# Hybrid decoder layer with expert retrieval, one core: the four-tap convolutions of blocks 1 and 2 move from VectorE to GpSimd

## What is computed

```python
def _causal_dwconv(x, buf, w):                 # width 4 for lru_x
    full = jnp.concatenate([buf.astype(x.dtype), x], axis=1)
    y = full[:, 0:s] * w[0]
    for k in range(1, width):
        y = y + full[:, k:k + s] * w[k]
    return y, full[:, full.shape[1] - (width - 1):]
...
    xc, new_lru_buf = _causal_dwconv(xl, lru_buf, lp['lru_conv_w'])
    xc = xc + lp['lru_conv_b']
    r = jax.nn.sigmoid(... w_rg_a ...); i = jax.nn.sigmoid(... w_rg_x ...)
    h = _linear_scan(a, bt, h0)                # bt uses i * xc
...
        act = jax.nn.gelu(jnp.einsum('td,thkd->thk', xb, u_tab[e]))
        return jnp.einsum('thk,thkd->td', g * act, v_tab[e])
```

## Time and profile before

| | us |
|---|---|
| three runs of the kernel | 3116.53, 3113.41, 3114.4 |
| their median | 3114.4 |
| the profiled execution, its time | 3113.92 |
| its span, first to last instruction | 3112.1 |

### The profile page before, as it was taken

How to read it: one execution, slowest core, us unless ns; L and a number is a source line. 1 busy time by engine, 2 the same in 40 slices (tenths; PEclk the granted TensorE clock), 3 DMA queues, 4 the chain that set the end, 5 groups by cost and what they waited for, 6 DMA issues and landing times. The chain is left out here.

```text
span 3112.1 us, 35134 instructions
## 1 busy us (share of the span) xinstructions
PE 2504.1 (80%) x10252; PEld 734.7 (24%) x10252; DVE 2146.2 (69%) x4925; ACT 1323.0 (43%) x4059; POOL 1273.2 (41%) x1092
## 2 busy tenths in 40 slices
PE   9989988898887997878867879876676666666776
PEld 5633322222221332223322223311111111110010
DVE  3676779888756477887776686676667666764554
ACT  2354455555435343554543353343333333333333
POOL 0034443444444444444444444444444444444443
PEclk9999999999997998999989879966776677777666
DMA  5489999999999999999999999999999999999997
GB/s 218 135 316 384 411 419 410 378 412 420 420 420 418 420 420 420 412 403 399 419 420 415 420 391 420 420 422 421 421 420 412 416 421 415 418 417 422 416 413 319
DMA packets 184150, 1236.40 MB, mean 397 GB/s; under 512 B 21011, under 2 KB 21267, under 8 KB 44179
## 3 DMA queue, kind: packets, MB, share of 16 engines
q0 software_dynamic: 156672, 1140.92, 89.0%
q1 hardware_dynamic: 27062, 92.58, 7.8%
q10 hardware_dynamic: 224, 0.66, 0.1%
HBM read 1226.91 MB, written 7.17 MB: 397 GB/s over the span
## 5 line engine op out<-in xcount | busy, mean ns | idle before, releaser
L731 POOL DMA_INDIRECT arena<-in_uv,idxT x1088 | 1273.0, 1170 | 1813.7 <-PE ps L1056 1570.2
L1742 DVE CUSTOM_DVE_ANT_0 arena<-arena 128x1024 f32<-128x1024 f32 x1088 | 1327.6, 1224 | 788.5 <-DMA arena<-in_uv,idxT 718.2
L1056 PE MATMUL ps<-arena,wset 128*32 128x512 f32 x4352 | 1372.3, 737 | 578.9 <-ACT wset L1306 570.1
L1301 ACT ACTIVATE gel<-acts 128x1 f32<-128x1 f32 x1088 | 219.0, 201 | 1427.1 <-DVE acts L1742 1422.1
L1056 PEld LDWEIGHTS ps<-arena,wset 128*32 128x32 f32 x4352 | 175.4, 118 | 1484.3 <-ACT wset L1306 1283.9
L1306 ACT ACTIVATE wset<-gated,gel 128x32 f32<-128x32 f32 x1088 | 349.6, 321 | 90.5 <-ACT gel L1301 1.8
L1299 ACT ACTIVATE gated<-arena,gT 128x32 f32<-128x32 f32 x1088 | 334.5, 307 | 0.1
L758 PE MATMUL ps<-arena 128*128 128x384 f32 (+1 forms) x768 | 306.5, 520 | 6.8 <-DMA arena<-in_w_in 6.8
L942 PE MATMUL ps<-arena 128*128 128x384 f32 (+3 forms) x896 | 287.3, 449 | 0.7 <-DVE small L1505 0.7
L1038 PE MATMUL ps<-arena 32*128 32x512 f32 x704 | 241.9, 769 | 1.3 <-ACT arena L1277 0.9
L942 PEld LDWEIGHTS ps<-arena 128*128 128x128 f32 x896 | 146.1, 190 | 199.0 <-issue 153.4
(11 more groups left out here) (189 smaller groups left out, 1555.6 us busy)
## 6 DMA issues: line engine op xcount, KB each, us to landing
arena<-in_wq SPq DMA_DIRECT2D x56, 512.0 KB
arena<-in_w_in SPq DMA_DIRECT2D x47, 512.0 KB
arena<-in_uv,idxT POOLq DMA_INDIRECT x1088
arena<-in_w_outs SPq DMA_DIRECT2D x24, 512.0 KB, 8.5
arena<-in_xT SPq DMA_DIRECT2D x4, 768.0 KB, 9.5
out_y<-arena SPq DMA_DIRECT2D x17, 128.0 KB
arena<-in_wkv SPq DMA_DIRECT2D x1, 2048.0 KB, 15.3
scratch_x<-arena SPq DMA_DIRECT2D x4, 512.0 KB, 3.3
```

What stands on the lines that cost most here:

```text
L731: pool.indirect_dma_start(out=ring[n % RING], out_offset=None, in_=A["uv"], in_offset=bass.IndirectOffsetOnAxis(ap=idxT[t % 2][:, col:col ...
L1056: last = mm(ps[r0:r0 + 32, hf * HALF:(hf + 1) * HALF], wset[n % SETS][:, :], v[:, hf * HALF:(hf + 1) * HALF], start=first, stop=final)
L1301: A_(gel[:, n % COLS:n % COLS + 1], acts[:, n % COLS:n % COLS + 1], ACT.Gelu).then_inc(gelus, 1)
L1742: V.tensor_tensor_reduce(out=ring[n % RING][:, 0:D], in0=ring[n % RING][:, 0:D], in1=xrep[g % 2], scale=1.0, scalar=0.0, op0=ALU.mult, op1 ...
```

## The change

The stage `cv` of blocks 1 and 2 is planned for GpSimd at the same slot numbers, and GpSimd gets a `stepper` of its own: after the request of slot n it calls `mix(n - RING + 1)`, so a piece that is due at slot v comes after the request of slot v + 7, one piece per slot. A convolution is five pieces: the small copies; the first tap (`tensor_scalar` with the bias); and three times a `tensor_scalar` into the buffer `rb` with a `tensor_tensor` that adds it to `xc` (GpSimd's form has two instructions per tap where VectorE had one). Every dependent pair has a wait on the new semaphore `pool_chain`. Block 0's convolutions stay on VectorE.

```diff
@@ plan_later_block
     for c in range(CL):
         x = o + 16 + 24 * c
-        put("dve", x + 9, b, "cv", c)
+        put("pool", x + 9, b, "cv", c)
...
@@ gpsimd
+        def run(b, name, arg):
+            n0, n_ = BLOCKS[b][1], cols(b)
+            xp, xs = parts(xl, 3, b)
+            kept = carry[:, arg * 3:(arg + 1) * 3]
+            after(pool, "act", b, "lx", arg)
+            if arg:
+                after(pool, "dve", b, "rc", arg - 1)
+            else:
+                after(pool, "dve", b - 1, "re", CL - 1)
+            did(G.tensor_copy(xl[:, 0:3], kept))
+            if b == 2:
...
+            else:
+                chain.wait()
+                did(G.tensor_copy(kept, xp[:, n0:n0 + 3]))
+            yield
+            for j in range(4):
+                wj = pcol("conv_w", arg * 4 + j)
+                sides = [(xc[arg % 2][:, 0:n0], xp[:, j:j + n0], rb[:, 0:n0])]
...
+                for o_, x_, t_ in sides:
+                    if j == 0:
+                        did(G.tensor_scalar(o_, x_, wj, pcol("conv_b", arg), ALU.mult, ALU.add))
+                    else:
+                        did(G.tensor_scalar(t_, x_, wj, None, ALU.mult))
+                chain.wait()
+                if j:
+                    did(G.tensor_tensor(xc[arg % 2][:, 0:n_], xc[arg % 2][:, 0:n_], rb[:, 0:n_], ALU.add))
+                    chain.wait()
+                if j == 3:
+                    pool.nop().then_inc(stage["pool"], 1)
+                yield
+
+        mix = stepper(PLAN["pool"], run, lambda b, name: 1)
         for n in range(NSLOT):
...
                 .then_inc(gath[n % RING], 16)
+            mix(n - RING + 1)
@@ tensor, stages gr and gi
-                after(pe, "dve", b, "cv", arg)
+                after(pe, conv_from(b), b, "cv", arg)
@@ scalar, stage lx
-                    after(act, "dve", b, "cv", arg - 1)
+                    after(act, conv_from(b), b, "cv", arg - 1)
@@ vector, stage rc
                 i_ = ib[arg % 2][:, 0:n_]
+                after(dve, conv_from(b), b, "cv", arg)
                 did(V.scalar_tensor_tensor(i_, i_, 1.0, xc[arg % 2][:, 0:n_], ALU.add, ALU.mult))
```

More of the change, by code:

```diff
@@ L103 @@
 G_MEM, G_LRU, G_SC = 0, 1, 2
-PLAN = {"pe": [], "act": [], "dve": [], "sp": []}
+PLAN = {"pe": [], "act": [], "dve": [], "sp": [], "pool": []}
 def stored(t):
@@ L294 @@
 plan_later_block(2)
-for _e in ("pe", "act", "dve"):
+for _e in ("pe", "act", "dve", "pool"):
     PLAN[_e].sort(key=lambda x: x[0])
@@ L305 @@
 APART = {"half", "ls", "K0", "Ka", "Kb", "T0", "E0", "S0", "I0", "G0", "R0", "C0"}
-DONE = {e: {} for e in ("pe", "act", "dve")}
+DONE = {e: {} for e in ("pe", "act", "dve", "pool")}
 for _e in DONE:
@@ L476, in build @@
     st_x1 = [sem(f"st_x1_{i}") for i in range(3)]
-    stage = {"pe": sem("pe_stage"), "act": sem("act_stage"), "dve": sem("dve_stage")}
+    stage = {"pe": sem("pe_stage"), "act": sem("act_stage"), "dve": sem("dve_stage"), "pool": sem("pool_stage")}
+    pool_c = sem("pool_chain")
     sq_mm, alpha_ready, prep_done, uexp_done, dve_c = sem("sq_mm"), sem("alpha_ready"), sem("prep_done"), sem("uexp_done"), sem("dve_chain")
@@ L498, in after, with conv_from @@
         eng.wait_ge(stage[who], DONE[who][(b, name, arg)])
+    def conv_from(b):
+        return "pool" if b else "dve"
     def z_from(b):
@@ L718, in _ @@
     def _(pool):
+        G = nc.gpsimd
+        chain = Chain(pool, pool_c)
+        did = chain.did
+        def run(b, name, arg):
[9 more added lines that the diff above has]
+            if b == 2:
+                pool.wait_ge(ld["cvst"], 16)
+                did(G.tensor_copy(xs[:, :, 0:3], cvst[:, arg * SB * 3:(arg + 1) * SB * 3]
+                                  .rearrange("p (s t) -> p s t", s=SB)))
+                at = SCOL["conv_p"] + arg * 3
+                did(G.tensor_copy(st[:, at:at + 3], xp[:, n0:n0 + 3]))
+                at = SCOL["conv_s"] + arg * SB * 3
+                did(G.tensor_copy(st[:, at:at + SB * 3].rearrange("p (s t) -> p s t", s=SB), xs[:, :, SS:SS + 3]))
+                chain.wait()
[6 more added lines that the diff above has]
+                sides = [(xc[arg % 2][:, 0:n0], xp[:, j:j + n0], rb[:, 0:n0])]
+                if b == 2:
+                    sides.append((xc[arg % 2][:, n0:n_].rearrange("p (s t) -> p s t", s=SB), xs[:, :, j:j + SS],
+                                  rb[:, n0:n_].rearrange("p (s t) -> p s t", s=SB)))
+                for o_, x_, t_ in sides:
[6 more added lines that the diff above has]
+                    did(G.tensor_tensor(xc[arg % 2][:, 0:n_], xc[arg % 2][:, 0:n_], rb[:, 0:n_], ALU.add))
+                    chain.wait()
+                if j == 3:
+                    pool.nop().then_inc(stage["pool"], 1)
+                yield
+        mix = stepper(PLAN["pool"], run, lambda b, name: 1)
         for n in range(NSLOT):
@@ L1405, in run @@
                 kept = carry[:, arg * 3:(arg + 1) * 3]
[L1406 to L1420, removed]
+                if arg == 0:
+                    did(V.memset(xl[:, 0:3], 0.0))
+                chain.wait()
+                did(V.tensor_copy(kept, xp[:, n0:n0 + 3]))
                 for _ in taps(xc[arg % 2], xl, 3, "conv_w", arg, pcol("conv_b", arg), b):
```

## The result

The changed kernel took 3144.85 us (median of six executions, 3138.34 to 3150.77), the kernel before 3114.36 (six, 3110.48 to 3116.53): a ratio of 1.0095, with a 95% interval from 1.0084 to 1.0106. That is 30.5 us more, outside the range of 3106 to 3128.

What follows compares the result with a forecast made beforehand. The prediction took the kernel as bound by its stream of gathers. From the profiled 3113.9 us it took 5.3 for VectorE's relief, added 2.6 for GpSimd's blocking, giving 3111.2, or 3111.7 as median; range 3106 to 3128.

Steps and rivals of the forecast that it cites:

- What bounds the kernel: Whole kernel: a stream of 1088 gathers, 2717 us of 3112.1; VectorE's work counts only where it returns ring buffers late.
- Removed from VectorE: Block 1's first two convolutions, 2.65 us each, repaid in starved stretches: gain 5.3 us; the other six worth nothing.
- The four stretches of the ceiling: At 540 to 560, 600 to 640 and 1400 to 1420, transfers miss 12.7 us together, the most a faster VectorE gives.
- the net term: Block 1's first two convolutions: 5.3 us gained from VectorE's relief, less 2.6 for what GpSimd takes.
- Added to GpSimd: Seven array instructions per block 1 convolution: 0.6 us per `tensor_scalar`, 0.9 per `tensor_tensor`, each dependent wait 0.12.
- What the two engines take from each other: Shared SBUF read interface: GpSimd delays VectorE 1.3 us per convolution, 2.6 us where it counts.
- GpSimd's own time: Tap slot at 480 to 640 takes 2.45 us against 1.68 spare; requests 2.3 us late after three taps, value taken 0.
- The library row: Between requests of slots 113 and 114: load of 1.28 to 15.3 us, low end taken, up to 10 covered.
- The new waits: TensorE's gate product after GpSimd's last tap, ending near 507: 0 to 2 us late, value taken 0.
- the cover: First convolution, block 1: 10 us between a request and its dot product, taken to hide late requests and TensorE's wait.
- rival 3: GpSimd too slow, at twice the prices: late requests at block 1's later convolutions and 1400 to 1420, +12, 3126; chance 0.18.
- `gr` waiting for GpSimd by more than 2 us each: Gate products: waits above 2 us each for GpSimd were listed among signs that the prediction is wrong.

Runs made afterwards that it cites:

- vector_late: Kernel before, all convolutions on VectorE, with gates, activations and recurrence of groups 0 to 2 of blocks 1 and 2 planned eight slots later: 3113.17 us, 0.9992.
- first_two: two_op_late with only block 1's first two convolutions on GpSimd, all others on VectorE; later slots stay: 3112.35 us, 0.9987 of the kernel before.
- gate_free: Changed kernel, but gate products and VectorE's `rc` product in blocks 1 and 2 read the keys instead of GpSimd's result: 3119.96 us, 1.001 of the kernel before.
- block2_only: Changed kernel with only block 2's four convolutions on GpSimd, block 1's on VectorE: 3121.63 us, 1.0015 of the kernel before.
- block1_only: Changed kernel with only block 1's four convolutions on GpSimd, block 2's on VectorE: 3138.76 us, 1.0064 of the kernel before.
- gates_late: Changed kernel with gates, activations and recurrence of groups 0 to 2 in blocks 1 and 2 planned eight slots later: 3128.33 us, 1.0042 of the kernel before.
- three_groups: two_op_late with group 3 of each block back on VectorE, six convolutions on GpSimd: 3114.12 us, 0.9992 of the kernel before.
- burst: Changed kernel with all five pieces of a convolution behind one request instead of five: 3140.55 us, 1.0078 of the kernel before.
- price_end: Kernel before with GpSimd's array instructions, four of each, added alone behind the last slot: 3145.71 us, one execution of a lengthened program.
- two_op: Changed kernel with GpSimd's tap product as a two-operation `tensor_scalar` (times the tap, plus 0.0): 3131.68 us, 1.0054 of the kernel before.
- two_op_late: Changed kernel with both edits, two_op's products and gates_late's later slots: 3121.37 us, 1.0019 of the kernel before.
- two_op_burst: burst with two_op's two-operation products: 3129.21 us, 1.0042 of the kernel before.

## Why the prediction was wrong

*What bounds the kernel* was right: the stream of gathers, and a VectorE that is behind at 480 to 640. The difference of the two blocks, from the earlier trace rows, was right too: equal waits cost four times as much in block 1.

*Removed from VectorE*, 5.3 us, less 2.6 for what GpSimd takes. The four stretches of the ceiling are no account to draw on. vector_late fills three of their places (423 and 420 GB/s at 600 to 640, 419 at 1400 to 1420) and takes nothing off VectorE, yet ends within the interval of no change, since over 480 to 720 it moves 403 GB/s where the kernel before moves 401: it has 373 and 382 at 560 to 600, before 395 and 419. Holes move; they are not a sum that can be collected. first_two against vector_late measures the net term: 0.8 us, where the prediction had 2.7. With eleven executions each, over 6.5 and 4.7 us, neither 0 nor 2.7 can be ruled out.

*Added to GpSimd*: `tensor_tensor` at 0.9 was right (0.991 alone). `tensor_scalar` at 0.6 was right for one of four and half of the truth for three (1.245 alone, 1.841 in place). My bounds of 0.47 to 2.54 held it.
The Trainium skill, GPSIMD Engine Reference, section Engine selection, calls operations with one input on GpSimd roughly line-rate; the measured 1.245 us with one operation stands against it, being more than the 0.991 of two inputs, while the 0.654 with two operations is nearer to VectorE's 0.471.

*What the two engines take from each other*: 1.3 us per convolution was close. VectorE's dot products in block 1 are longer by

```profile
L1784 DVE CUSTOM_DVE_ANT_0 arena<-arena 128x1024 f32<-128x1024 f32 x92 | 116.9, 1283 | 14.2 <-DMA arena<-in_uv,idxT 10.4 <-DVE arena L1556 1.3 <-DVE arena L1469 0.8
```

at 480 to 760, against, before, at 480 to 730,

```profile
L1742 DVE CUSTOM_DVE_ANT_0 arena<-arena 128x1024 f32<-128x1024 f32 x90 | 109.1, 1220 | 17.7 <-DMA arena<-in_uv,idxT 14.1 <-DVE arena L1514 1.3 <-DVE arena L1428 1.0
```

so 92 x 0.063 = 5.8 us over four convolutions, 1.4 each on the dot products alone. The other direction was under-sized: GpSimd's one-operation products stood 0.6 each and the gathers of the first convolution 0.7 each (1.62 to 1.70 instead of 0.94), and that, with the product's own 1.245, is what stretched the convolution.

*GpSimd's own time*, 2.45 us for a tap slot, was 3.4 us at first (501.00 to 504.43), then 3.2 and 2.4, so requests came later than I had it. But the value taken, 0, was nearly right: gate_free shows no shift from slot 104 to the end, and 1.6 us at most on the way.

*The library row*: no delay that a run shows; the trace has two records of 39 ns for it at 496.7. In block2_only the first `tensor_scalar` behind it began 0.1 us after these records and took 0.78 us.

*The new waits* is the step that failed. "GpSimd's last tap follows a request at about 502, and ends near 507: TensorE, the additions and so `used` are late by 0 to 2 us, under the same cover of 10; value taken 0." Two things were wrong in it. The first is its size. The pieces come one per request, so each piece's lateness moves the next request, and the five add up: the request ahead of the last tap came at 509.87, 8 us late, and the tap ended at 513.96, 7 us late. The eight convolutions took 17.6 to 22.6 us, and the eight waits 5.0 to 8.9. The second is the cover. The 10 us that I gave it are between a request and the dot product on its rows. They cover a late *request*. A wait on TensorE does not start there: it stops the score products and VectorE's search behind them, or ScalarE's tanh and VectorE's recurrence behind it, and with either the dot products on rows that have already landed, on the engine that is late in this stretch. Nothing covers that. block1_only, gate_free, gates_late and three_groups show it from four sides. With the waits, block 1 costs 22.9 us. Without them the dot products shift from slot 104 to 168 by 1.5 us (a free input), -1.1 (room in the plan) and -5.2 (room and two-operation products). The control of the last two has -5.1, so the most that any of them loses is 4.0.

*The rivals*: rival 3 had the price, 3.03 us for the pair of instructions in place against its 3.0, and the direction, but not the path. It let late requests reach the DMA queues, for +12; burst is the kernel in which that happens, and there it costs 25. The condition in the last line of the prediction, "`gr` waiting for GpSimd by more than 2 us each", named the true sign, and no rival had been worked out from it.

What stays open: how much VectorE's relief is worth by itself; why GpSimd's one-operation `tensor_scalar` costs 0.6 us more than the one with two, and where the 4.1 us between gate_free's median and that of the kernel before lie; its interval reaches down to 0.3.

## What to carry to other kernels

When work moves to a slower engine, find its first consumer and what stands behind that consumer in the same list, before pricing anything else: here a wait of 7 us before one matmul stopped a second engine's search or recurrence, and with it the stream, while the slow work itself cost some 4 us or less. Cover is a property of one path: time in hand for a late transfer is no time in hand for a late operand. Work done in pieces, one per turn of a loop, ends late by the sum of all pieces' delays, and the plan must give its readers that room; and a control that moves only the readers is needed before the move itself is credited.

## What the runs showed of the hardware

GpSimd's `tensor_scalar` over 128x384 took 1.245 us with one operation and 0.654 with two (price_end); adding a second operation that does nothing brought 13 us of 3145 (two_op).

GpSimd can stand for a whole series of VectorE's instructions, not for one. In two_op_late, with a second operation in it and thus 0.65 us of work,

```profile
498.05 5.49 POOL L759 TENSOR_SCALAR arena<-arena,par 128x384 f32<-128x384 f32 x1
```

while VectorE's timeline has four dot products nearly end to end:

```profile
498.01 1.21 DVE L1787 CUSTOM_DVE_ANT_0 arena<-arena 128x1024 f32<-128x1024 f32 x1
...
499.49 1.20 DVE L1787 CUSTOM_DVE_ANT_0 arena<-arena 128x1024 f32<-128x1024 f32 x1
...
500.63 1.21 DVE L1787 CUSTOM_DVE_ANT_0 arena<-arena 128x1024 f32<-128x1024 f32 x1
...
501.88 1.20 DVE L1787 CUSTOM_DVE_ANT_0 arena<-arena 128x1024 f32<-128x1024 f32 x1
```

It ended 0.46 us behind the fourth. Between them VectorE ran only short reads of its sum, a copy of 0.41 us and a cast of 0.17. This is GpSimd's first `tensor_scalar`, behind the library row, but that row does not explain it: the 5.32 us of two_op_burst, at the same place in VectorE's list, fell on its third, while the first had taken 1.55. Four more kernels have a 5.5 us `tensor_scalar` at this place (block1_only, gates_late, three_groups, first_two). It is not the rule: in the changed kernel the one at 496.86 met dot products from 496.14, 497.28 and 498.55, and ended after 2.18 us, ahead of the end of the third. The other direction shows as well: in the changed kernel the dot product that began at 503.52, 0.09 us after a GpSimd addition, took 1.99 us and ended 1.08 after it.
The Trainium skill, SBUF — State Buffer, section Who interferes with whom, says that whichever of the two starts second stands until the first is done. The dot product of 1.99 us agrees; that GpSimd did not get its turn between four dot products, for 5.49 us, goes beyond what it says.
